# The recurrence's loop: one 128-column product of the state for z and the outputs, in place of two of 64

## What is computed

```python
def step(state, inp):
    r_t, w_t, k_t, v_t, kk_t, a_t = inp
    sa = jnp.einsum('bhvk,bhk->bhv', state, -kk_t)
    state = (state * w_t[:, :, None, :] + sa[..., None] * (kk_t * a_t)[:, :, None, :]
             + v_t[..., None] * k_t[:, :, None, :])
    return state, jnp.einsum('bhvk,bhk->bhv', state, r_t)
```

## Time and profile before

| | us |
|---|---|
| median of 3 runs | 4401.06 |
| lowest, highest | 4398.26, 4411.34 |
| the profiled execution's own time | 4397.11 |
| its span in the trace | 4395.3 |
| mean granted clock of TensorE | 0.943 |

### The profile page before, as it was taken

One profiled execution on the slowest core, in us unless ns is written; L12 is line 12 of the kernel. 1 busy time (PEld: TensorE's weight loads), 2 busy tenths in 40 slices (PEclk: granted clock), 3 DMA queues, 4 the chain that ended last, 5 costly groups with the idle time before them and its releaser, 6 DMA issues. The chain is left out here.

```text
span 4395.3 us, 50269 instructions
## 1 busy us (share of the span) xinstructions
PE 4023.3 (92%) x20175; PEld 3134.3 (71%) x20175; DVE 2200.5 (50%) x3220; ACT 1661.2 (38%) x2270; POOL 139.8 (3%) x246
## 2 busy tenths in 40 slices
PE   5699999789799799977889999999995899999998
PEld 2466657668688688634677788888885777888887
DVE  6611123463544764375555555455547455554554
ACT  4221112341343444322224454354443445544543
POOL 2000000000000000002110000000000000000000
PEclk8799999899999999997769999999997999999999
DMA  9566555203265166532325565665561555656664
GB/s 355 184 214 206 196 183 172 92 24 120 72 192 166 64 213 196 158 115 90 117 84 169 145 186 191 187 185 188 189 219 59 183 175 144 186 190 189 186 198 162
DMA packets 351933, 719.05 MB, mean 164 GB/s; under 512 B 24478, under 2 KB 26874, under 8 KB 346858
## 3 DMA queue, kind: packets, MB, share of 16 engines
q1 hardware_dynamic: 331872, 637.74, 46.3%
q0 software_dynamic: 18192, 76.35, 5.1%
q10 hardware_dynamic: 1672, 2.24, 0.1%
HBM read 686.33 MB, written 26.48 MB: 162 GB/s over the span
## 5 line engine op out<-in xcount | busy, mean ns | idle before, releaser
L2187 DVE TENSOR_TENSOR ring_r<-ring,ring_r 128x1024 fp32r<-128x1024 f32 (+1 forms) x984 | 1189.6, 1218 | 1677.7 <-ACT ring_r L1496 1653.9
L1496 ACT ACTIVATE ring_r<-ring 128x1024 fp32r<-128x1024 f32 (+1 forms) x984 | 1029.6, 1053 | 1796.3 <-DMA ring<-in_w_in 587.2
L862 PE MATMUL acc<-ring_r,feat_hi 128*128 128x512 f32 x5120 | 1598.9, 394 | 32.3 <-DVE modc L2569 14.7
L862 PEld LDWEIGHTS acc<-ring_r,feat_hi 128*128 128x128 f32 x5120 | 956.5, 189 | 282.9 <-issue 32.1
L862 PE MATMUL acc<-ring_r,feat_lo 128*128 128x512 f32 x2560 | 1000.3, 391 | 0.0
L862 PE MATMUL acc<-ring_r,hid_t_hi 128*128 128x512 f32 x2048 | 631.5, 390 | 0.0
L862 PEld LDWEIGHTS acc<-ring_r,feat_lo 128*128 128x128 f32 x2560 | 482.7, 189 | 102.6
L862 PEld LDWEIGHTS acc<-ring_r,hid_t_hi 128*128 128x128 f32 x2048 | 383.7, 188 | 79.3
L862 PE MATMUL acc<-ring_r,hid_t_lo 128*128 128x512 f32 x1024 | 398.5, 389 | 0.0
L862 PE MATMUL acc<-ring_r,feat_e_hi 128*128 128x512 f32 (+1 forms) x1088 | 332.2, 388 | 17.1 <-DVEq L2275 9.8
L862 PEld LDWEIGHTS acc<-ring_r,feat_e_hi 128*128 128x128 f32 x1088 | 204.7, 191 | 58.3 <-issue 12.0
(11 more groups left out here) (453 smaller groups left out, 3268.4 us busy)
## 6 DMA issues: line engine op xcount, KB each, us to landing
ring<-in_ffn_up SPq DMA_DIRECT2D x256, 512.0 KB, 3.7
ring<-in_ffn_down SPq DMA_DIRECT2D x256, 512.0 KB, 3.9
ring<-in_w_mod SPq DMA_DIRECT2D x192, 512.0 KB, 5.4
ring<-in_w_in SPq DMA_DIRECT2D x176, 512.0 KB, 3.8
ring<-in_w_out SPq DMA_DIRECT2D x64, 512.0 KB, 3.7
ring<-in_even_w_in SPq DMA_DIRECT2D x64, 512.0 KB, 3.6
ring<-in_xattn_wkv SPq DMA_DIRECT2D x32, 512.0 KB, 5.4
ring<-in_even_w_out SPq DMA_DIRECT2D x32, 512.0 KB, 3.6
```

The source lines that it names most:

```text
L862: mm = pe.matmul(bank[0:l.shape[-1], 0:width], l, r, start=(kk == 0 and j == 0), stop=(kk == g.kt - 1 and j == len(terms) - 1))
L1496: f(ring_r[:, slot, 0, 0:kt, 0:width], ring[:, slot, 1, 0:kt, 0:width], ACT.Copy) \
L2187: tt(lo, raw, hi, ALU.subtract).then_inc(sem("w_lo"), E.up("w_lo"))
```

## The change

The blocks `w_a2` and `w_r2` become one block, `w_ar2`, with 128 columns for each pair of heads. In Z, for c > 0, one product of 128 columns reads the state: columns 0 to 63 give z in rows 0 to 63, columns 64 to 127 give the outputs' first part in rows 64 to 127 of the same bank. The bank belongs to ACT then, and O later accumulates its eight products by `G[:, 1]` onto rows 64 to 127 of it, with no bank of its own. The round of the banks stays as it was. ACT spreads all four parts of `w_ar2` behind W, ahead of `w_t2` and `w_b2`, and none behind its copy of O; the copy takes rows 64 to 127. The wait ahead of O for `bd_ready` goes. In the first turn the products are the same as before.

```diff
-        w_a2 = view(28448, 8, 2, RC)
-        w_r2 = view(28960, 8, 2, RC)
+        w_ar2 = view(28448, 8, 2, 2, RC)
...
-                        w_o[RC * o:RC * o + RC, c % 2].rearrange("p (h d) -> p h d", d=B_D), f"o_out{c % 2}")
+                        w_o[2 * RC + RC * o:2 * RC + RC * o + RC, c % 2].rearrange("p (h d) -> p h d", d=B_D), f"o_out{c % 2}")
...
-                    both_heads("dve_free", low, lambda hp: ([(flat(w_a2[:, hp]), old[:, hp])] if c else []) + [(flat(G[low, 0, hp]), v[low, hp])])
+                    bank = begin("act_free")
+                    for hp in range(8):
+                        cols = slice(hp * B_D, (hp + 1) * B_D)
+                        if c:
+                            pe.matmul(bank[:, cols], flat(w_ar2[:, hp]), old[:, hp], start=(hp == 0), stop=False)
+                        mm = pe.matmul(bank[low, cols], flat(G[low, 0, hp]), v[low, hp], start=not c, stop=not c or hp == 7)
+                    mm.then_inc(sem("unit_full"), E.up("unit_full"))
...
                     if c < NRC - 1:
-                        both_heads("dve_free", full, lambda hp: [(flat(w_kb2[c % 2][:, hp]), v[:, hp])])
-                    if c:
-                        pe.wait_ge(sem("bd_ready"), E.due("bd_ready"))
-                    both_heads("act_free", low, lambda hp: ([(flat(w_r2[:, hp]), old[:, hp])] if c else []) + [(flat(G[:, 1, hp]), v[:, hp])])
+                        both_heads("dve_free", full, lambda hp: (flat(w_kb2[c % 2][:, hp]), v[:, hp]))
+                        owners.append(owners[-4])
+                    for hp in range(8):
+                        mm = pe.matmul(bank[high, hp * B_D:(hp + 1) * B_D], flat(G[:, 1, hp]), v[:, hp], start=not c, stop=not c or hp == 7)
+                    mm.then_inc(sem("unit_full"), E.up("unit_full"))
...
-                        spread(lambda o: w_a2[ks[o], :, o], lambda o: w_ar[ks[o], :, c + 1, 0])
+                        for j in range(2):
+                            spread(lambda o: w_ar2[ks[o], :, j, o], lambda o: w_ar[ks[o], :, c + 1, j])
...
-                    f(w_o[0:2 * RC, c % 2], take("unit_full")[0:2 * RC, :], ACT.Copy).then_inc(sem("act_free"), E.up("act_free"))
+                    act.wait_ge(sem("unit_full"), E.due("unit_full"))
+                    f(w_o[2 * RC:4 * RC, c % 2], both[2 * RC:4 * RC, :], ACT.Copy).then_inc(sem("act_free"), E.up("act_free"))
...
-                    if c < NRC - 1:
-                        spread(lambda o: w_r2[ks[o], :, o], lambda o: w_ar[ks[o], :, c + 1, 1])
-                        bd_ready()
...
-                    dve.tensor_copy(w_z[low], take("unit_full")[low, :]).then_inc(sem("dve_free"), E.up("dve_free"))
+                    dve.tensor_copy(w_z[low], take("unit_full")[low, :]).then_inc(sem("dve_step"), E.up())
```

More of the change, by code:

```diff
@@ L1251, in both_heads @@
                     for hp in range(8):
-                        terms = products(hp)
-                        for j, (lt, rhs) in enumerate(terms):
-                            mm = pe.matmul(bank[rows, hp * B_D:(hp + 1) * B_D], lt, rhs, start=(j == 0), stop=(j == len(terms) - 1))
+                        lt, rhs = products(hp)
+                        mm = pe.matmul(bank[rows, hp * B_D:(hp + 1) * B_D], lt, rhs, start=True, stop=True)
                     mm.then_inc(sem("unit_full"), E.up("unit_full"))
@@ L1259, in within @@
                 def within(c):
-                    both_heads("dve_free", full, lambda hp: [(flat(w_b2[:, hp]), flat(w_ar[:, hp, c]))])
+                    both_heads("dve_free", full, lambda hp: (flat(w_b2[:, hp]), flat(w_ar[:, hp, c])))
                 pe.wait_ge(sem("bd_ready"), E.due("bd_ready"))
@@ L1274, in rwkv @@
                         pe.wait_ge(sem("bd_ready"), E.due("bd_ready"))
-                    both_heads("dve_free", low, lambda hp: ([(flat(w_a2[:, hp]), old[:, hp])] if c else []) + [(flat(G[low, 0, hp]), v[low, hp])])
+                    bank = begin("act_free")
[5 more added lines that the diff above has]
+                    mm.then_inc(sem("unit_full"), E.up("unit_full"))
                     pe.wait_ge(sem("zu_ready"), E.due("zu_ready"))
                     pe.wait_ge(sem("bd_ready"), E.due("bd_ready"))
-                    both_heads("dve_free", high, lambda hp: [(flat(w_t2[low, hp]), w_z[low, hp * B_D:(hp + 1) * B_D])])
+                    both_heads("dve_free", high, lambda hp: (flat(w_t2[low, hp]), w_z[low, hp * B_D:(hp + 1) * B_D]))
                     if c < NRC - 1:
@@ L1853, in even @@
             def even():
+                nonlocal g_n
                 g_in, g_uq, g_qi, g_uv, g_kv0, g_kv1, g_out = gemms["even"]
@@ L1964, in even @@
                     round_hi(g_out.q0 + c)
+                    both = acc[g_n % 4]
                     if c < NRC - 1:
@@ L1974, in even @@
                         skip("unit_full", 1)
+                        g_n += 1
                     else:
@@ L3115, in rwkv @@
                         dve.nop().then_inc(sem("st_ready"), E.count("st_ready"))
+                        g_n += 1
                     take_lo(g_out.q0 + c)
-                    skip("unit_full", 1)
+                    E.seen["unit_full"] += 1
                     if c in (2, 4):
```

## The result

| | before | changed |
|---|---|---|
| median of 7 runs each, us | 4402.27 | 4420.5 |
| ratio of the changed to before, 95% interval | | 1.0038 (1.0024 to 1.0052) |
| span of the profiled execution, us | 4395.3 | 4415.8 |
| seven turns, first U to last U, us | 122.85 | 139.16 |

The account below looks back on a forecast made before the run. TensorE was taken to bound the loop. Seven turns of 19.87 us at clock 0.50 make 139.1 us, 16.2 more than 122.85; added to 4399.7, the mean of two lower runs, this gave 4415.9, range 4402 to 4423.

Parts of the forecast that it names:

- TensorE bounds the loop: In the seven turns: TensorE busy for 116.89 of 122.85 us, idle only some 0.8 us a turn.
- A merged product costs as much as the two it replaces: State reads in Z: one 128-column product costs two of 64 columns, 0.426 against 0.213 each; O loses what Z gains.
- A change of shape costs 0.19 us: In Z, 16 changes between 128-column and 64 x 64 products at 0.19 us each, with 0.14 and 0.30 as ends.
- The clock no longer rises behind a short O: All seven turns stay at clock 0.50, losing the 13.98 us that rises behind the long O saved before.
- Nothing waits for the state or the spreads: Ahead of Z, the state is ready with 0.4 us to spare and ACT's eight spreads end in time; cost nothing.
- The last O's gain is hidden behind DVE's chain: In the last turn O loses 1.77 us, but nobody waits for its end; at most a gain of 1.8.
- The sum: Whole change: seven turns of 19.87 us make 139.1, 16.2 us more than 122.85; forecast 4415.9.
- the clock's rise in every turn: Rival for the loop: the clock still rises once a turn, so the change costs 2 us, 4402; chance 0.12.
- a new wait: Rival in Z: state or block comes late, at 0.5 us a turn 3.5 us more, 4419.5; chance 0.04.
- The second rival: The clock rises in some turns only, each giving back 2 to 2.5 us: +5 to +13, 4405 to 4412; chance 0.13.
- The product of 128 columns at 0.213 us: Rival in Z: S is slow for another reason than width, so Z is 6.45 us, +4.3 us, 4404; chance 0.06.

Follow-up runs that it names:

- experiment 6: Changed kernel with each 128-column product in Z issued as two of 64 columns, into low and high rows; ratio 1.0013, loop 126.8 us.
- experiment 1: Changed kernel with Z sorted by shape, the eight 128-column products first, then the eight of 64 x 64; ratio 1.0002, loop 121.1 us.
- experiment 4: Kernel before without O's eight products by `w_r2`, so O is short in every turn; ratio 1.0014, loop 126.2 us.
- experiment 3: Changed kernel with each of O's eight products issued twice for c > 0, making O long again; ratio 1.0047, loop 138.8 us.
- experiment 2: Kernel before with Z sorted by shape, the eight products by `w_a2` first, then the eight of 64 x 64; ratio 0.9959, loop 97.1 us.
- 8: Kernel before with Z sorted and W's and S's 128-column products split, all low rows first, then all high rows; ratio 0.9909, loop 85.4 us.
- 7: Kernel before with Z sorted and W's and S's 128-column products split in two, low and high rows in turn; ratio 0.9886, loop 70.7 us.

## Why the prediction was right

- *TensorE bounds the loop.* Right: DVE, ACT and POOL kept their busy times, and only TensorE's grew.
- *A merged product costs as much as the two it replaces.* Right for this change: Z took 8.16 us where 8.16 were computed, O 1.90, W and S as before, a turn 19.88 against 19.87. (The long O of 3.67 us is 0.07 more than 16 x 0.213 + 0.19, so "exactly" was a little strong; nothing hung on it.) What the prediction did not see is that two products of 64 columns need not follow each other: in different halves they run at once (experiment 6). Before the change they stood in different steps and in the same rows.
- *A change of shape costs 0.19 us, also from 128 columns to 64 x 64, for which there was no row.* Right: the value taken, and neither end of 0.14 and 0.30, gives the 8.16 us; experiment 1 shows it again.
- *The clock no longer rises behind a short O.* Right, and the heart of the loss: 0.50 in all seven turns. Experiment 4 shows it with nothing else changed, experiment 3 the other way round. The price was right as well: 13.98 us reckoned for the rises before, which experiment 4 gives too, and 16.3 for the whole loop.
- *Nothing waits for the state or the spreads.* Right: the state was ready 0.38 us ahead of Z, where 0.4 was reckoned.
- *The last O's gain is hidden behind DVE's chain.* Right: 9.38 us from the last U to DVE's first copy behind the loop, before and after.
- *The sum.* 16.2 us; the loop shows 16.3 and the ratio 0.38%, which is 17 us. That they agree to 0.1 us is luck: beside the second trace of the kernel before (a loop of 120.7) the changed loop is 18.5 us longer. The forecast of 4415.9 lay 4.6 us under the median of 4420.5, for I had set the sum on the mean of two low runs; on the median of before, 4402.27, it gives 4418.5.

The rivals: the clock's rise in every turn or in some did not come about in the changed kernel, although TensorE was busy for 19.05 of 19.88 us in a turn, nor did a new wait. The second rival's sum was loose: two or three turns at 2 to 2.5 us give back 4 to 7.5, which makes +9 to +12 and not +5 to +13. The product of 128 columns at 0.213 us did not come about either; two of 64 in different halves have that price.

## What to carry to other kernels

Before merging small products, look up what a product costs in the trace by the width of its weights: where two of 64 columns cost what one of 128 does, the merge saves nothing, and the gain lies in issuing the two into different halves, right behind each other, and in sorting products by shape. And where a loop runs below the full clock, ask which stretch raises it: taking work out of that stretch can cost more than the work did. Read the granted clock turn by turn, not the busy share alone.

## What the runs showed of the hardware

- Two products of 128 rows by 64 columns into rows 0 to 63 and 64 to 127 of one bank start at the same 0.01 us in the timeline and take the time of one (experiment 6). W as eight wide products takes 3.60 us at a clock of 0.50, as eight narrow ones into the low rows and then eight into the high ones 3.24, and with low and high in turn 1.92 (experiments 2, 8 and 7).
- Of two loops with nearly the same busy share of TensorE (19.05 of 19.88 us a turn in the changed kernel, 16.93 of 17.76 before), one had a clock of 0.50 throughout and in the other it rose in every turn but the first. With sorted products the clock stayed at 1.00 through a turn of 9.70 us in which TensorE waited 0.8 us for z (experiment 2). Busy time alone does not tell the clock.
- Less work can take more time: 48 products left out, 3.4 us more (experiment 4); 48 added, and in the traced execution no more time than without them (experiment 3). Why the clock did not rise in two of experiment 3's turns stays open.
